# A Strassen-type product of seven blocks for half of the second MLP matrix, with strips and column groups in turn

## The chip, the cores and the metric

One core of a Trainium2 chip runs the whole program. The metric is the device time of one execution in microseconds; lower is better. The kernel before takes 2650.49 us (median of three runs, 2650.14 to 2651.08).

## What is computed

Two transformer-like blocks on 256 tokens of width 2048, in fp32. The change touches only the MLP of the first:

```
ff = square(relu(h @ mlp_w1 + mlp_b1))          # 256 x 2048 by 2048 x 8192
h  = layer_norm(ALPHA * h + ff @ mlp_w2 + mlp_b2)   # 256 x 8192 by 8192 x 2048
```

Ahead of it stand a recurrent and a convolutional mixer; behind it attention, a convolution and a second, gated MLP.

## The kernel before

fp32 accuracy comes from splitting. Every operand a is rounded to `hi` (type fp32r, which TensorE takes in one pass) and `lo` = a - `hi`; a product is `hi*hi + hi*lo + lo*hi`, three passes added up in PSUM. The activations are split once, the weights as they stream through.

**The ring of weights.** A *piece* is 128 x 1024 weights, 512 KB. Four slots (`RING`) hold a raw, a high and a low copy: `w_raw`, `w_hi`, `w_lo`. Piece r (0 to 3) of *quad* q goes through slot r: SyncE loads it (`quad`, L284) once `lo` of the piece before in that slot is done; ScalarE rounds it (`split`, L889 in the rows) once it has landed and TensorE has left the slot (`pe_piece`); VectorE subtracts (`lo`, L1373); TensorE waits for both (`piece_ready`) and counts `pe_piece` up at the end. Every engine takes its work strictly in the order written out by hand in its block.

**The MLP** takes quads 74 to 137, in eight rounds i of 8 quads (`mlp`, on TensorE L652, with functions of the same name on ScalarE and VectorE). A round makes 1024 hidden features and multiplies them with 1024 rows of the second matrix, W2:

- two *strips* of 512 features, 8 pieces each (`strip`): weights are stationary, 512 columns (the tokens' `hi` and `lo`) pass for `w_hi` (L395) and 256 for `w_lo` (L406). Strip k=0 is summed in PSUM half GB, k=1 in GA. At its end ScalarE copies the `lo` part (`halves`, L900, into `half`), VectorE adds it, the rest and the bias (L1777, four steps), squares (L1783), ScalarE rounds (`hi_of`, L904, into `ff`) and VectorE subtracts (`lo_of`, L1397);
- four *column blocks* n of W2, 512 columns each (`token_pieces`, L504 to L506): `ff` of 128 features by 128 tokens is stationary, 512 columns of a piece pass. A piece is two feature tiles of one n, so 2 tiles x 2 token halves x 3 = 12 passes. Each n has two banks (`W2_BANKS`), 8 feature tiles and four pieces; two n share two quads. At the end VectorE adds the banks to `zt` (`add_tokens`, L1766).

In round 0 TensorE also turns the start values of `zt` between the column pieces (`turn_seed`), which ScalarE keeps (`keep_seed`). After the last round come the statistics of the norm (`strip_stats`), a few passes on zeros (`keep_busy`), the turning of the result, and strip 138.

## Time and profile before

| | us |
|---|---|
| median of 3 runs | 2650.49 |
| profiled execution, first to last instruction | 2647.7 |
| MLP, first strip to last column block (trace) | about 893 to 1597 |
| TensorE busy | 2631.6 |
| VectorE busy | 1745.8 |
| ScalarE busy | 1362.4 |

PE is TensorE's matmul, PEld its weight loads (they overlap matmuls), DVE is VectorE, ACT ScalarE, POOL GpSimd, SP SyncE. The matmul ends are modelled (a pass shown as 0.39 us is followed by the next after less), so the distance between starts is what a pass costs. The same holds for VectorE: the next instruction starts a little before the shown end of the one before, unless it must wait for its result. "Idle before <-X" names what an engine waited for.

### The profile page before, as it was taken

To read this page: it belongs to the slowest core of one execution; us is meant where nothing else is said; L and a number is where in the kernel's file an instruction comes from. 1 tells how busy PE (TensorE), PEld (TensorE's weight loads), DVE (VectorE), ACT (ScalarE), POOL (GpSimd) and SP (SyncE) were. 2 spreads that over 40 slices of the span, in tenths; PEclk is the share of its full clock that TensorE was granted. 3 is DMA by queue.
4 is the path that set the end of the run, shared out by engine and by line. 5 is a ranking of instruction groups with operands and counts; after the bars stand their busy time and mean duration, and the time that the engine had idled before them with its cause. 6 is when DMAs were issued, how large, how long until landed. Compare 5 with 4: busy or idle time off the path is not lost.

```text
span 2647.7 us, 40522 instructions
## 1 busy us (share of the span) xinstructions
PE 2631.6 (99%) x14379; PEld 2279.8 (86%) x14379; DVE 1745.8 (66%) x1863; ACT 1362.4 (51%) x1588; POOL 36.1 (1%) x30
## 2 busy tenths in 40 slices
PE   9999999999999999999999999999999999999999
PEld 8888888888888888888888888878888888888888
DVE  7787877544455655555555568996666666666667
ACT  5767765444444544444444445587554444444444
POOL 0000000000000100000000001000100000000000
PEclk9999999999999999999999999999999999999999
DMA  7555555555656455556555664534555555555554
GB/s 266 181 186 184 191 186 195 197 182 189 201 198 199 160 187 193 176 192 202 192 178 193 198 195 153 177 129 147 171 191 190 188 186 188 190 190 190 190 190 168
DMA packets 133881, 494.01 MB, mean 187 GB/s; under 512 B 14864, under 2 KB 15376, under 8 KB 133776
## 3 DMA queue, kind: packets, MB, share of 16 engines
q1 hardware_dynamic: 133776, 492.62, 56.4%
q8 instruction: 65, 1.06, 0.2%
q14 instruction: 40, 0.33, 0.0%
HBM read 490.46 MB, written 2.10 MB: 186 GB/s over the span
## 4 chain that ended last, share of the span: by engine, by line
PE 92%; DVE 3%; ACT 2%; issue 2%; DMA 0%; DVEq 0%; SPq 0%; ACTq 0%
PE ps_b L395 18%; PE ps_a L395 18%; PE ps_b L406 10%; PE ps_a L406 10%; PE ps_b L504 6%; PE ps_b L506 6%; PE ps_b L505 6%; PE ps_a L505 5%; PE ps_a L504 5%; PE ps_a L506 5%; DVE w_lo L1373 1%; PE ps_b L826 1%; ACT w_hi L889 1%; DVE bconv L1874 1%; DVE gates L1519 1%
## 5 line engine op out<-in xcount | busy, mean ns | idle before, releaser
L1373 DVE TENSOR_TENSOR w_lo<-w_raw,w_hi 128x1024 fp32r<-128x1024 f32 (+1 forms) x908 | 1120.4, 1251 | 726.3 <-ACT w_hi L889 716.9
L889 ACT ACTIVATE w_hi<-w_raw 128x1024 fp32r<-128x1024 f32 (+1 forms) x908 | 966.9, 1075 | 1105.1 <-PE ps_a L506 237.1
L395 PE MATMUL ps_b<-xx,w_hi 128*128 128x512 f32 x1184 | 287.9, 392 | 4.0 <-DVE xx L1690 2.3
L395 PE MATMUL ps_a<-xx,w_hi 128*128 128x512 f32 x1120 | 269.1, 391 | 0.0
L395 PEld LDWEIGHTS ps_b<-xx,w_hi 128*128 128x128 f32 x1184 | 216.9, 188 | 47.7 <-ACT w_hi L889 3.7
L395 PEld LDWEIGHTS ps_a<-xx,w_hi 128*128 128x128 f32 x1120 | 205.8, 188 | 39.8
L395 PE MATMUL ps_a<-x,w_hi 128*128 128x512 f32 x704 | 165.9, 390 | 0.0
L395 PE MATMUL ps_b<-x,w_hi 128*128 128x512 f32 x704 | 165.5, 390 | 0.0
L406 PEld LDWEIGHTS ps_b<-xx,w_lo 128*128 128x128 f32 x1184 | 153.2, 192 | 5.8
L406 PE MATMUL ps_b<-xx,w_lo 128*128 128x256 f32 x1184 | 156.0, 284 | 0.0
L395 PEld LDWEIGHTS ps_b<-x,w_hi 128*128 128x128 f32 x704 | 130.8, 188 | 26.2
L395 PEld LDWEIGHTS ps_a<-x,w_hi 128*128 128x128 f32 x704 | 130.6, 188 | 26.1
L406 PEld LDWEIGHTS ps_a<-xx,w_lo 128*128 128x128 f32 x1120 | 142.3, 191 | 4.4
L406 PE MATMUL ps_a<-xx,w_lo 128*128 128x256 f32 x1120 | 144.4, 283 | 0.0
L504 PE MATMUL ps_b<-w_hi,xx 128*128 128x512 f32 (+1 forms) x320 | 122.6, 383 | 0.0
L506 PE MATMUL ps_b<-w_hi,xx 128*128 128x512 f32 (+1 forms) x320 | 121.3, 379 | 0.0
L505 PE MATMUL ps_b<-w_lo,xx 128*128 128x512 f32 (+1 forms) x320 | 121.3, 379 | 0.0
L504 PE MATMUL ps_b<-w_hi,ff 128*128 128x512 f32 x256 | 99.9, 390 | 0.0
L506 PE MATMUL ps_b<-w_hi,ff 128*128 128x512 f32 x256 | 99.6, 389 | 0.0
L505 PE MATMUL ps_b<-w_lo,ff 128*128 128x512 f32 x256 | 99.6, 389 | 0.0
L504 PE MATMUL ps_a<-w_hi,ff 128*128 128x512 f32 x256 | 99.6, 389 | 0.0
L505 PE MATMUL ps_a<-w_lo,ff 128*128 128x512 f32 x256 | 99.6, 389 | 0.0
(305 smaller groups left out, 3933.5 us busy)
## 6 DMA issues: line engine op xcount, KB each, us to landing
w_raw<-w_dram SPq DMA_DIRECT2D x836, 512.0 KB, 3.4
w_raw<-w_dram SPq DMA_DIRECT2D x72, 640.0 KB, 3.9
zz<-x_dram SPq DMA_DIRECT2D x8, 256.0 KB, 4.6
x_res<-x_dram SPq DMA_DIRECT2D x4, 512.0 KB, 6.0
out_dram<-res SPq DMA_DIRECT2D x3, 512.0 KB, 2.8
out_dram<-res SPq DMA_DIRECT2D x4, 128.0 KB, 2.1
const<-const_dram SPq DMA_DIRECT2D x1, 449.0 KB, 4.5
prm<-prm_dram SPq DMA_DIRECT2D x1, 308.0 KB, 5.4
```

What stands on the lines that cost most here:

```text
L395: last = nc.tensor.matmul(group[:, j, :], w_hi[:, r, o * P:o * P + P], moving(src, at + k), start=begins and k == 0, stop=not begins and k ...
L406: last = nc.tensor.matmul(group[:, j, 0:S], w_lo[:, r, o * P:o * P + P], moving(src, at + k)[:, 0:S], start=begins and k == 0, stop=not be ...
L504: nc.tensor.matmul(dst, x_hi, hi, start=k == 0 and not begun, stop=False)
L505: nc.tensor.matmul(dst, x_hi, lo, start=False, stop=False)
L506: last = nc.tensor.matmul(dst, x_lo, hi, start=False, stop=k == kt - 1)
L826: nc.tensor.matmul(banks[:, j // 2, (j % 2) * S:(j % 2) * S + S], w_hi[:, r, cols], mix_tile(k)[:, half_at:half_at + S], start=False, stop ...
L889: act.activation(w_hi[:, r, 0:width], w_raw[:, r, 0:width], ACT.Copy).then_inc(hi_done, 1)
L1373: dve.tensor_tensor(w_lo[:, r, 0:width], w_raw[:, r, 0:width], w_hi[:, r, 0:width].bitcast(F32), ALU.subtract).then_inc(lo_even if r % 2 = ...
L1519: own.done(dve.tensor_tensor_scan(gates[:, hd, way, 0, order], aa[:, way, hd, order], tt[:, way, hd, order], 0.0, ALU.mult, ALU.add))
L1874: ins = dve.scalar_tensor_tensor(y, x, column("cv_w", n), y, ALU.mult, ALU.add)
```

## The change

In rounds i = 1 to 6, and for the second pair of column blocks of round 0, the feature tiles 2 to 5 of the 8 are no longer multiplied block by block. Two feature tiles x two token halves on the left, two feature tiles x two column blocks (two whole pieces) on the right make a 2 x 2 by 2 x 2 block product, done with seven block products instead of eight (`seven_products`, called twice in each `grouped`: g=0 for tiles 2, 3 in slots 2 and 3 of the first quad, g=1 for tiles 4, 5 in slots 0 and 1 of the second). Each block product is three passes of 512 columns. Tiles 0, 1, 6, 7 go as before, before and after. Four results (m1, m5, m6, m7) are summed in GB, and per group added to `q_acc`; m2, m3, m4 go straight into the banks of the plain products in GA. `combined` puts `q_acc` into `zt` once for each pair, at the end.

The sums of blocks that this needs:

- of weights, on VectorE (`mixed_pieces`): a sum of 512 written over the first half of the odd raw piece, a difference of 512 and a difference of 1024, to `t_raw`; then ScalarE rounds 1536 elements (`t_high`) and VectorE subtracts (`t_low`), twice a group;
- of `ff`, four of 256 elements once a round (`next_inputs_of`), rounded and subtracted (`s_hi`, `s_lo`).

The order changes too. A pair of column blocks (a *group*: the 8 pieces of two quads) and a strip alternate, strips are always in GB (but for strip 76), and the strips are made one half round ahead. A strip waits until `q_acc` has taken the group's results out of GB (`q_kept`); a group's seven products wait until the strip's sums are out. The loads come in another order (`by_groups`), with the same bytes. VectorE's order in a group is that of `strip_end` and `group_end`. Round 7 has plain products from its own `ff_last`. GpSimd clears `q_acc` once.

```diff
+        t1_made, t_made, t_hi, t_lo, t_used = (sem(n) for n in ("t1_made", "t_made", "t_hi", "t_lo", "t_used"))
+        s_made, s_hi, s_lo = sem("s_made"), sem("s_hi"), sem("s_lo")
+        q_zero, q_out, q_kept = sem("q_zero"), sem("q_out"), sem("q_kept")
...
+        def product_operands(g, wh, wl, r0, buf):
+
+            r1, k = 2 * (r0 // 2) + 1, 2 * g + 2
+
+            def tile(k, t):
+                return ff[:, k, t * P:t * P + P], ff[:, k, S + t * P:S + t * P + P]
+
+            def summed(n):
+                return s_hi_of[:, n, g * P:g * P + P], s_lo_of[:, n, g * P:g * P + P]
+
+            def piece(r, h):
+                return wh[:, r, 512 * h:512 * h + 512], wl[:, r, 512 * h:512 * h + 512]
+
+            def mixed_piece(n):
+                return thi[:, buf, 512 * n:512 * n + 512], tlo[:, buf, 512 * n:512 * n + 512]
+
+            return dict(m1=(GB[:, 0, :], tile(k, 0), piece(r0, 0)),
+                        m2=(GA[:, 0, :], tile(k + 1, 0), piece(r0, 1)),
+                        m3=(GA[:, 2, :], summed(3), piece(r1, 1)),
+                        m4=(GA[:, 1, :], tile(k + 1, 1), mixed_piece(2)),
+                        m5=(GB[:, 1, :], summed(0), piece(r1, 0)),
+                        m6=(GB[:, 2, :], summed(1), mixed_piece(0)),
+                        m7=(GB[:, 3, :], summed(2), mixed_piece(1)))
 
...
+
+            strip_quads(74, 224)
+            strip_quads(76, 232)
+            strip_quads(78, 256)
+            strip_quads(80, 240)
+            strip_quads(82, 264)
+            by_groups(84, 248)
+            strip_quads(86, 288)
+            with sp.Fori(0, 5) as i:
+                q, at = 8 * i + 88, 32 * i + 256
+                by_groups(q, at + 16)
+                strip_quads(q + 2, at + 40)
+                by_groups(q + 4, at + 24)
+                strip_quads(q + 6, at + 64)
+            by_groups(128, 432)
+            strip_quads(130, 456)
+            by_groups(132, 440)
+            with sp.Fori(0, 8) as i:
+                quad(i + 134, w8, 4 * i + 464, N8)
...
+            def up_strip(q, e, free):
+                strip(q, e, GB, xx, KT, nothing, free=free, by_pairs=True)
+
+            def product(operands, begins, ends):
+
+                bank, (a_hi, a_lo), (b_hi, b_lo) = operands
+                nc.tensor.matmul(bank, a_hi, b_hi, start=begins, stop=False)
+                nc.tensor.matmul(bank, a_hi, b_lo, start=False, stop=False)
+                return nc.tensor.matmul(bank, a_lo, b_hi, start=False, stop=ends)
+
+            def seven_products(i, g, done, q, r0):
+
+                m = product_operands(g, w_hi, w_lo, r0, g)
+                piece_ready(q, r0)
+                product(m["m1"], g == 0, g == 1)
+                product(m["m2"], False, False).then_inc(pe_piece, 1)
+                piece_ready(q, r0 + 1)
+                product(m["m5"], g == 0, g == 1)
+                product(m["m3"], False, False).then_inc(pe_piece, 1)
+                pe.wait_ge(t_hi, done + g + 1)
+                pe.wait_ge(t_lo, done + g + 1)
+                product(m["m6"], g == 0, g == 1)
+                last = product(m["m7"], g == 0, g == 1)
+                if g == 1:
+                    last.then_inc(q_out, 1)
+                product(m["m4"], False, False).then_inc(t_used, 1)
+
+            def grouped(i, pair, q):
+
+                n = 2 * i + pair
+                need = need_ff(2 * i)
+                for nn in range(2):
+                    pe.wait_ge(acc_out, 2 * n - 1 + nn)
+                    token_pieces([(q, nn, two_tiles(0))], sums_of(nn), ff, 8, need)
+                pe.wait_ge(strip_out, outs(E_MLP + 2 * i + 3 + pair))
+                pe.wait_ge(s_hi, i + 1)
+                pe.wait_ge(s_lo, i + 1)
+                seven_products(i, 0, 2 * n - 2, q, 2)
+                need(4)
+                seven_products(i, 1, 2 * n - 2, q + 1, 0)
+                for nn in range(2):
+                    token_pieces([(q + 1, 2 + nn, two_tiles(6))], sums_of(nn), ff, 8, nothing)
...
+            def mlp(i):
+
+                q, e = 8 * i + 80, E_MLP + 2 * i + 3
+                grouped(i, 0, q)
+                up_strip(q + 2, e, lambda: pe.wait_ge(q_kept, 4 * i))
+                grouped(i, 1, q + 4)
...
+            strip(74, E_MLP, GB, xx, KT, need_normed(0), free=lambda: pe.wait_ge(z_kept, 3), turns=False)
+            strip(76, E_MLP + 1, GA, xx, KT, nothing)
+            up_strip(78, E_MLP + 2, lambda: pe.wait_ge(strip_out, outs(E_MLP + 1)))
+            pe.wait_ge(strip_out, outs(E_MLP + 2))
+            in_order(80, sums_of, ff, need_ff(0), beside=seeds_beside)
+            up_strip(82, E_MLP + 3, lambda: pe.wait_ge(seed_kept, 4))
+            grouped(0, 1, 84)
+            up_strip(86, E_MLP + 4, lambda: pe.wait_ge(q_kept, 2))
+            with pe.Fori(0, 5) as i:
                 mlp(i + 1)
-
...
+            mlp(6)
+            pe.wait_ge(q_kept, 26)
+            in_order(134, lambda nn: W2_BANKS[nn], ff_last, need_ff(14))
+            in_order(136, sums_of, ff_last, nothing, begin=lambda nn: pe.wait_ge(acc_out, 27 + nn), apart=z_half)
+
+            pe.wait_ge(acc_out, 30)
...
+            def split_group(n, q, r0):
+
+                split(q, r0)
+                act.wait_ge(t1_made, n + 1)
+                split(q, r0 + 1)
+
+            def t_high(n, buf):
+                hi_of(thi[:, buf, :], t_raw[:, buf, :], t_made, n + 1, t_hi)
+
+            def ff_high(dst, i, k):
+                hi_of(dst[:, 4 * k:4 * k + 4, 0:S], hid[:, k, :, :], ff_made, 2 * i + k + 1, ff_hi)
+
+            def strip_end(q, e, k, sums, n):
+
+                splits(q + 2, N8, (0, 1))
+                split_group(n, q + 2, 2)
+                if sums is not None:
+                    act.wait_ge(s_lo, sums + 1)
+                halves(e, 4 * q + 8, GB)
+                t_high(n, 0)
+
+            def group_end(q, n):
+
+                split_group(n + 1, q + 1, 0)
+                t_high(n + 1, 1)
+                splits(q + 1, N8, (2, 3))
+                splits(q + 2)
+
+            def next_inputs_of(i):
+
                 for k in range(2):
...
+                act.wait_ge(s_made, i + 1)
+                act.activation(s_hi_of, half[:, :, :], ACT.Copy).then_inc(s_hi, 1)
+
+            def mlp(i):
+
+                q, n = 8 * i + 80, 4 * i - 2
+                group_end(q, n)
+                splits(q + 3)
+                strip_end(q + 2, E_MLP + 2 * i + 3, 1, None, n + 2)
+                group_end(q + 4, n + 2)
+
...
+            def mixed_pieces(n, q, r0, buf):
+
+                even, odd = w_raw[:, r0, 0:N8], w_raw[:, r0 + 1, 0:N8]
+                made = t_raw[:, buf, :]
+                dve.wait_ge(raw_in[r0], 16 * q + 16)
+                dve.wait_ge(raw_in[r0 + 1], 16 * q + 16)
+                dve.tensor_tensor(odd[:, 0:512], even[:, 0:512], odd[:, 0:512], ALU.add).then_inc(t1_made, 1)
+                if not (isinstance(n, int) and n < 2):
+                    dve.wait_ge(t_used, n - 1)
+                dve.wait_ge(t1_made, n + 1)
+                own.done(dve.tensor_tensor(made[:, 0:512], odd[:, 0:512], odd[:, 512:N8], ALU.subtract))
+                own.need()
+                dve.tensor_tensor(made[:, 512:1536].rearrange("p (h c) -> p h c", h=2),
+                                  even.rearrange("p (h c) -> p h c", h=2),
+                                  made[:, 0:512].unsqueeze(1).to_broadcast([P, 2, 512]), ALU.subtract).then_inc(t_made, 1)
+
+            def t_low(n, buf):
+                lo_of(tlo[:, buf, :], t_raw[:, buf, :], thi[:, buf, :], n + 1, t_hi, t_lo)
...
+            def strip_end(q, i, k, n):
+
+                e = E_MLP + 2 * i + k
+                los(q + 2, N8, (0, 1))
+                mixed_pieces(n, q + 2, 2, 0)
+                lo(q + 2, 2)
+                activated(e, i, k, GB)
+                lo(q + 2, 3)
+                squared(e + 1, k)
+                t_low(n, 0)
+
+            def group_end(q, pair, n, done):
+
+                mixed_pieces(n + 1, q + 1, 0, 1)
+                los(q + 1, N8, (0, 1))
+                t_low(n + 1, 1)
+                los(q + 1, N8, (2, 3))
+                los(q + 2, N8, (0, 1))
+                dve.wait_ge(q_out, done + 1)
+                for h in range(2):
+                    dve.tensor_tensor(q_acc[:, pair, 2 * h:2 * h + 2, :], GB[:, 2 * h:2 * h + 2, :],
+                                      q_acc[:, pair, 2 * h:2 * h + 2, :], ALU.add).then_inc(q_kept, 1)
+                lo(q + 2, 2)
+                add_sums(pair, 0, 4 * q + 7)
+                lo(q + 2, 3)
+                add_sums(pair, 1, 4 * q + 8)
+
+            def next_inputs_of(i, q):
+
+                dve.wait_ge(ff_made, 2 * i + 2)
+                h = pairs[:, 1:3, :, :, :]
+                one, two, three_, four = (s_sum[:, n, :, :] for n in range(4))
+                own.done(dve.tensor_tensor(one, h[:, :, 0, 1, :], h[:, :, 1, 1, :], ALU.add))
+                own.need()
+                own.done(dve.tensor_tensor(two, one, h[:, :, 0, 0, :], ALU.subtract))
+                own.need()
+                own.done(dve.tensor_tensor(three_, h[:, :, 0, 1, :], h[:, :, 0, 0, :], ALU.subtract))
+                dve.tensor_tensor(four, h[:, :, 1, 0, :], two, ALU.subtract).then_inc(s_made, 1)
+                ff_low(ff, i, 0)
+                lo(q + 1, 0)
+                ff_low(ff, i, 1)
+                lo(q + 1, 1)
+                lo_of(s_lo_of, half[:, :, :], s_hi_of, i + 1, s_hi, s_lo)
+                los(q + 1, N8, (2, 3))
...
+            def combined(pair):
+
+                q = q_acc[:, pair, :, :]
+                dve.wait_ge(q_kept, 24 + 2 * pair)
+                dve.wait_ge(acc_out, 26 + 2 * pair)
+                own.done(dve.tensor_tensor(q[:, 2, :], q[:, 0, :], q[:, 2, :], ALU.add))
+                own.need()
+                own.done(dve.tensor_tensor(q[:, 3, :], q[:, 2, :], q[:, 3, :], ALU.add))
+                own.need()
+                own.done(dve.tensor_tensor(zt[:, :, 2 * pair, :], zt[:, :, 2 * pair, :], q[:, 0:4:3, :], ALU.add))
+                own.need()
+                own.done(dve.tensor_tensor(q[:, 2:4, :], q[:, 1:2, :].to_broadcast([P, 2, 512]), q[:, 2:4, :], ALU.subtract))
+                own.need()
+                own.done(dve.tensor_tensor(zt[:, :, 2 * pair + 1, :], zt[:, :, 2 * pair + 1, :], q[:, 2:4, :], ALU.add))
...
+            def mlp(i, between=None):
+
+                q, n = 8 * i + 80, 4 * i - 2
+                group_end(q, 0, n, 2 * i - 1)
+                if between is not None:
+                    between()
+                los(q + 3)
+                strip_end(q + 2, i + 1, 1, n + 2)
+                group_end(q + 4, 1, n + 2, 2 * i)
...
+            lo(82, 0)
+            dve.wait_ge(seed_kept, 1)
+            add_sums(0, 0, 4 * 81 + 2)
+            los(82, N8, (1, 2))
+            dve.wait_ge(seed_kept, 2)
+            add_sums(0, 1, 4 * 82)
+            lo(82, 3)
+            los(83)
+            dve.wait_ge(seed_kept, 4)
+            strip_end(82, 1, 1, 0)
+            dve.wait_ge(q_zero, 1)
+            group_end(84, 1, 0, 0)
+            next_inputs_of(1, 86)
+            strip_end(86, 2, 0, 2)
+            with dve.Fori(0, 5) as i:
+                own.enter(i, 7)
                 mlp(i + 1)
-            mlp(7, last=True)
+                next_inputs_of(i + 2, 8 * i + 94)
+                strip_end(8 * i + 94, i + 3, 0, 4 * i + 6)
+                own.leave(5)
+            ff_low(ff_last, 7, 0)
+
+            def first_pair():
+                combined(0)
+
+            mlp(6, first_pair)
+            ff_low(ff_last, 7, 1)
...
+            lo(136, 0)
+            add_last(0, None, 4 * 135 + 2)
+            los(136, N8, (1, 2))
...
                 last.then_inc(res_seed, 1)
+            pool.wait_ge(seed_kept, 4)
+            pool.memset(q_acc[:, :, :, :], 0.0).then_inc(q_zero, 1)
```

## Rows read from the trace of the kernel before

**Rows 1.** The page: busy time of each engine, share of the span, instructions

```profile
PE 2631.6 (99%) x14379; PEld 2279.8 (86%) x14379; DVE 1745.8 (66%) x1863; ACT 1362.4 (51%) x1588; POOL 36.1 (1%) x30
```

**Rows 2.** Stretches: length, busy time (instructions) by engine, granted clock, DMA share, GB/s

```profile
core 0: us, PE busy (x) PEld busy (x) DVE busy (x) ACT busy (x) POOL busy (x), PEclk, DMA share, GB/s
...
1152.00:1240.00 88.00, 88.00 (x450) 75.44 (x449) 50.78 (x49) 37.05 (x36) 0.00 (x0) 1.00 0.58 190
```

**Rows 3.** Waits from 896 to 1600: who for whom, total, times, longest

```profile
DVE w_lo L1373 <- ACT w_hi L889: 233.1, 132, 3.4
ACT w_hi L889 <- PE ps_a L506: 102.7, 62, 3.0
```

**Rows 4.** Timeline of PE, 1240 to 1285: start, length, line, operation, count

```profile
1239.64 0.39 PE L506 MATMUL ps_a<-w_hi,ff 128*128 128x512 f32 x1
...
1245.08 0.39 PE L506 MATMUL ps_a<-w_hi,ff 128*128 128x512 f32 x1
1245.30 3.79 PE L395 MATMUL ps_b<-xx,w_hi 128*128 128x512 f32 x16
...
1267.53 3.79 PE L395 MATMUL ps_a<-xx,w_hi 128*128 128x512 f32 x16
```

**Rows 5.** Timeline of DVE at the end of that strip; in brackets idle before

```profile
1269.90 1.66 DVE L1777 SCALAR_TENSOR_TENSOR hid<-ps_b,prm,half 128x256 f32<-128x256 f32 x4 [1.58 <-ACT half L900]
1271.48 1.22 DVE L1373 TENSOR_TENSOR w_lo<-w_raw,w_hi 128x1024 fp32r<-128x1024 f32 x1
1272.61 1.22 DVE L1783 SCALAR_TENSOR_TENSOR hid<-hid 128x1024 f32<-128x1024 f32 x1
...
1298.33 3.49 DVE L1373 TENSOR_TENSOR w_lo<-w_raw,w_hi 128x1024 fp32r<-128x1024 f32 x3
```

**Rows 6.** Timeline of DVE, 1592 to 1599: steps that need the one before

```profile
1592.03 1.23 DVE L1766 TENSOR_TENSOR zt<-ps_a,zt 128x1024 f32<-128x1024 f32 x1 [0.41 <-PE ps_a L506]
1593.29 1.29 DVE L1663 BATCH_NORM_STATS2 stats<-zt 128x6 f32<-128x512 f32 x2
...
1597.46 0.69 DVE L1766 TENSOR_TENSOR zt<-ps_a,zt 128x512 f32<-128x512 f32 x1 [0.28 <-PE ps_a L506]
1598.19 0.69 DVE L1663 BATCH_NORM_STATS2 stats<-zt 128x6 f32<-128x512 f32 x1
```

**Rows 7.** Groups by shape, whole span: count, busy us, mean ns, idle before

```profile
L1373 DVE TENSOR_TENSOR w_lo<-w_raw,w_hi 128x1024 fp32r<-128x1024 f32 x836 | 1014.4, 1231 | 659.1 <-ACT w_hi L889 651.6 <-DVE hid L1385 3.4 <-DVE padded L1385 1.9
L1373 DVE TENSOR_TENSOR w_lo<-w_raw,w_hi 128x1280 fp32r<-128x1280 f32 x72 | 106.1, 1490 | 67.2 <-ACT w_hi L889 65.3 <-issue 1.7
...
L1397 DVE TENSOR_TENSOR xx<-zz,xx 128x512 fp32r<-128x512 f32 x8 | 5.5, 686 | 2.6 <-ACT xx L908 2.6
...
L1397 DVE TENSOR_TENSOR mixc<-ps_a,mixc 128x256 fp32r<-128x256 f32 x8 | 3.4, 419 | 0.0
...
L889 ACT ACTIVATE w_hi<-w_raw 128x1280 fp32r<-128x1280 f32 x72 | 91.7, 1274 | 98.2 <-PE ps_a L506 52.9 <-PE ps_a L448 11.1 <-PE ps_b L448 9.3
```

**Rows 8.** Timeline of ACT at the end of the same strip

```profile
1267.79 1.06 ACT L889 ACTIVATE w_hi<-w_raw 128x1024 fp32r<-128x1024 f32 x1 [0.81 <-PE ps_b L395]
1268.75 1.01 ACT L900 ACTIVATE half<-ps_b 128x1024 f32<-128x1024 f32 x1
```

**Rows 9.** Timeline, 1608 to 1612: TensorE stands and starts again

```profile
1609.87 1.67 DVE L1690 SCALAR_TENSOR_TENSOR xx<-res,prm,xx 128x256 fp32r<-128x256 f32 x4
...
1611.69 0.70 PE L395 MATMUL ps_b<-xx,w_hi 128*128 128x512 f32 x2 [2.31 <-DVE xx L1690]
```

**Rows 10.** DMA issues by tile: count, KB each, median us to landing

```profile
w_raw<-w_dram SPq DMA_DIRECT2D x836, 512.0 KB, 3.4
```

**Rows 11.** Stretches around that start, columns as in rows 2

```profile
1612.00:1614.00 2.00, 2.00 (x8) 1.60 (x7) 2.00 (x2) 2.00 (x5) 0.00 (x0) 0.77 0.00 0
1614.00:1616.00 2.00, 2.00 (x11) 1.99 (x10) 1.85 (x5) 0.99 (x2) 0.00 (x0) 0.50 0.77 268
1616.00:1618.00 2.00, 2.00 (x13) 1.82 (x12) 0.82 (x2) 1.06 (x1) 0.00 (x0) 0.87 0.74 231
```

More of the change, by code:

```diff
@@ new lines, in in_order @@
+            def in_order(q, banks, src, need, begin=None, beside=None, apart=None):
+                for c in range(2):
+                    for nn in range(2):
+                        if c == 0 and begin is not None:
+                            begin(nn)
+                        pieces = [(q + c, 2 * nn + h, two_tiles(4 * c + 2 * h)) for h in range(2)]
+                        if apart is not None and (c, nn) == (1, 1):
+                            token_pieces(pieces, banks(nn), src, 8, need, apart)
+                            continue
+                        for _, r, runs in pieces:
+                            if beside is not None:
+                                beside(c, r)
+                            token_pieces([(q + c, r, runs)], banks(nn), src, 8, need)
@@ new lines, in mlp @@
+            def mlp(i):
[4 more added lines that the diff above has]
+                group_end(q + 4, n + 2)
+            splits(76)
+            halves(E_MLP, 4 * 74 + 8, GB)
+            splits(77)
+            splits(78)
+            halves(E_MLP + 1, 4 * 76 + 8, GA)
+            next_inputs_of(0)
+            splits(79)
+            splits(80)
+            act.wait_ge(s_lo, 1)
@@ new lines, in _ @@
+            halves(E_MLP + 2, 4 * 78 + 8, GB)
+            splits(81, N8, (0, 1))
+            keep_seed(0)
+            split(81, 2)
+            keep_seed(1)
+            split(81, 3)
+            split(82, 0)
+            keep_seed(2)
+            split(82, 1)
+            keep_seed(3)
+            splits(82, N8, (2, 3))
+            splits(83)
+            strip_end(82, E_MLP + 3, 1, None, 0)
+            group_end(84, 0)
+            next_inputs_of(1)
+            splits(87)
+            strip_end(86, E_MLP + 4, 0, 1, 2)
@@ new lines, in t_low, with activated @@
+            def t_low(n, buf):
+                lo_of(tlo[:, buf, :], t_raw[:, buf, :], thi[:, buf, :], n + 1, t_hi, t_lo)
+            def activated(e, i, k, group):
+                dve.wait_ge(half_out, e + 1)
+                for j in range(SN):
+                    ins = dve.scalar_tensor_tensor(hid[:, k, j, :], group[:, j, 0:S],
+                                                   column("b1", 4 * k + j + 8 * i), half[:, j, :], ALU.add, ALU.add)
+                ins.then_inc(strip_out, 1)
```

235 lines of the change are left out of this document (105 added, 130 removed).

## The prediction

> **What bounds the kernel now.** I read the busy table first: TensorE is busy for 99% of the span [rows 1], so every pass taken away is worth its length if nothing takes its place. The stretch table then shows a steady stretch of the MLP, 88 us, one round of two strips and four W2 column blocks: TensorE is busy throughout at granted clock 1.00, VectorE for 50.78 us (58%), ScalarE for 37.05 us [rows 2]. The waits between 896 and 1600 us hold no row of TensorE; what waits is VectorE for `w_hi` (233.1 us in all), and ScalarE for TensorE to give a slot back [rows 3]. So VectorE has spare time on average. Whether it has some at the place where the change needs it is the question, and the timelines answer that.
>
> The clock of the sum: from the start at 1239.64 to that at 1245.08 lie 24 passes of 512 columns [rows 4], so one pass is 5.44 / 24 = 0.2267 us. A strip goes from 1245.30 to 1267.53, 22.23 us [rows 4]. A pair of column blocks (8 pieces of 12 passes, quads q and q+1) is 96 x 0.2267 = 21.76 us. Strip and pair together are 43.99 us, and two of these are 88.0 us, the round.
>
> **What goes away.** `seven_products` has 7 x 3 passes for two pieces instead of 24, and each `grouped` call has two of it: 6 passes less, 90 instead of 96, 1.36 us. `grouped` runs 13 times (`grouped(0, 1)`, and twice each for i = 1 to 6); i = 7 and the first pair of i = 0 keep eight products. TensorE's work shrinks by 78 x 0.2267 = 17.7 us. The order of strips and groups, the loads (same bytes, other order), `w_hi` and `w_lo` stay otherwise.
>
> **What VectorE gets.** Prices are distances from start to start: a 1024-element difference costs 1.135 us in a run (3.50 us for three, the last counted with its 1.23 in full) [rows 5]. A step that needs the result before it starts after the whole duration: a 512-element one 0.73 us later (1597.46 to 1598.19), a 1024-element one 1.26 us [rows 6]. For 1536 elements there is no row. The nearest are 128x1024 with 1.231 and 128x1280 with 1.490 us [rows 7]; from 512 to 1024 the slope gives 1.231 + 0.545 = 1.78, from 1024 to 1280 1.75. Bounds: 1.490 below (a bit more than 1280 elements), 2 x 1.231 above; I take 1.77, that is 1.675 to the next start. One such step stands in the chain below, 13 times in all: the lower end would make the time 3.6 us shorter, the upper 9.0 us longer, and the range holds both. `mixed_pieces` is 0.73 + 0.73 + 1.14 = 2.60 us, and a pair has two; `t_low` 1.675, two; `q_acc` two PSUM additions of 1.14 us; `next_inputs_of` four sums of 256 elements, 0.42 us long each [rows 7], and one `s_lo`. A strip with its group comes to 16 x 1.135 (the `lo`), 1.58 + 1.14 (bias, square), 5.20, 3.35, 2.27, 2.27 (adding into `zt`) and half of 5.0 (`next_inputs_of`, once in two): 37.5 us of 42.6, or 88%. On average that fits. ScalarE gets two `t_high` and half an `s_hi`, about 3.4 us in 42.6; it has room.
>
> **Where it doesn't fit.** Let T be TensorE's first pass after a strip (1267.53 in the trace). VectorE can't take the strip's sums before ScalarE has `half`: split at 1267.79, `half` at 1268.75, VectorE's first bias step at 1269.90 [rows 5, 8], T + 2.37. That won't move, since in `strip_end` the split of the last slot stands before `halves` as before. From there, in the order of `strip_end` and `group_end`: four bias steps 1.58, `lo(q+2, 3)` 1.13, square 1.14, `t_low` 1.675, `mixed_pieces` of the second block set 2.60, then `lo` of that set's first piece, 1.23 to its end. That is T + 2.37 + 9.36 = 11.73, and TensorE starts again some 0.15 us after VectorE's end (1609.87 + 1.67 = 11.54 against 11.69 [rows 9]): T + 11.88. TensorE wants this piece after two plain pieces and seven products, 24 + 21 = 45 passes: T + 10.20. It stands still for 1.68 us, and behind that `piece_ready` all of its later work is queued.
>
> The other waits of the group: the first `t_low` ends at T + 7.99, wanted at 36 passes = T + 8.16: just in time, and if it slips, that only eats into the 1.68. The second goes at 12.78 (ScalarE's `t_high` before it, from 10.7 to about 12.2, by 1.27 us for 1280 elements [rows 7]) and ends at 14.54, wanted at 11.88 + 12 passes = 14.60; with 0.15 to resume this is a stall of 0.09. `lo` of slots 2 and 3 end at 15.7 and 16.8, wanted at 16.7 and 19.4: nothing. `q_acc` follows two more `lo` and ends near T + 21.35, and the next strip waits for it; TensorE gets there at 11.88 + 0.09 + 45 x 0.2267 = T + 22.17. Nothing, but only 0.8 us of room. In the strip (22.23 us) VectorE has 8 `lo`, the `zt` sums and perhaps `next_inputs_of`; it is through `mixed_pieces` and `lo` of slot 2 by about T + 1.0, before the T + 2.37 at which the chain starts anew. So nothing piles up. Of the four raw blocks loaded in that time the last is issued at about 14 to 15 us into the strip and lands 3.4 us later [rows 10], ahead of its sums at 19.4.
>
> **The sum.** Group before 21.76, after 22.17: +0.41 us. So 13 x 0.41 = +5.3 us: a saving of 17.7 and stalls of 23.0. Once, `combined(1)` (two dependent steps of 0.73, three of 1.26, 5.2 us) stands before quad 135: at the start of quad 134 VectorE still owes 2 `lo`, two sums and an `ff_low`, so the first `lo` of 135 ends 11.3 us in, wanted after 48 passes = 10.9: +0.55. `combined(0)` and the first `next_inputs_of` stand beside strips with 4 us and more to spare: nothing, and were that cover gone, 5 us and 1 us once. Pool's memset stands beside a strip of which VectorE needs `q_acc` only afterwards: nothing, at most its own few us once. Sum +5.9 us on the profiled span of 2647.7; the median of the runs is 2650.49, 2.8 above it, and I carry that over: 2656.4.
>
> A rule against the row: the Trainium skill, VectorE: DVE Perf Modes, Terms, says that a VectorE instruction can't issue until the pipeline of the one before is empty. By it the four bias steps and three big ones of the chain would each be 0.09 us longer, some 0.6 us a group, 8 us in all, and the time 2664. The trace doesn't agree: three steps of 1.23 us take 3.50, not 3.69 [rows 5].
>
> **Rivals.** *A stall that costs the clock (slower).* The trace has one idle stretch of 2.31 us before 1611.69, and right behind it the granted clock is 0.77 and then 0.50, the lower of the levels 1.2 and 2.4 GHz, where it was 1.00 before; it is back at 1.00 by 1618 [rows 9, 11]. The clock was short by 2 x (0.23 + 0.50 + 0.13), 1.7 us. If my 1.68 us stalls do that in half of the groups, 6.5 x 1.7 = 11 us more: 2667; in each, 2678. Against it: the stall is shorter and dense passes stand on both sides. The Trainium skill, TensorE: Matmul & The Clock Gate, HAM oscillation, has the same rule, that an idle gap inside a loop throttles again each round; the trace agrees for its one gap. The same event at the end of the MLP may also come or stay away, 1.7 us.
> *The strip waits for `q_acc` (slower).* SyncE issues the first piece of the next strip only after that late `lo`; if blocks land over 4.5 us after issue instead of the 3.4 of the median, `lo` of slots 0 and 1 and with them `q_acc` slip past T + 22.1. At 5 us it is 0.5 us a group: 2663.
> *The saving is kept (faster).* If VectorE reached the second set's `lo` 1.5 us earlier (steps on SBUF alone cheaper than I price them, by half), nothing would stall but the 21.4 us of `q_acc`, 0.4 us better than before a group: 2646; with that gone too, 2633. Against it: rows on SBUF and on PSUM cost the same 1.22 to 1.23 us, and all of the chain's first half is in the trace. In between lies a part: each step 0.05 us cheaper, 2650.
>
> **How the numbers follow.** About 0.2% (5.3 us, so 2645.2 to 2655.8) is what a measurement of this kernel can tell from no change. My chain as it stands, 2653 to 2660: 0.60, of which 0.25 within 0.2%. Clock: 0.10. `q_acc`: 0.10. Saving kept: 0.10 faster. The part in between: 0.10, same. So faster 0.10, same 0.35, slower 0.55. Range 2648 to 2668: it leaves out the kept saving and the worst of the clock.
>
> **What would show it.** TensorE's waits should name VectorE's `w_lo` 13 times, 1.4 to 1.9 us each, at the first pass of the second block set, and `tlo` with 0.2 us or less. Groups should be 22.2 us from strip end to strip start, with VectorE without a gap from T + 2.4 to T + 21. If groups are near 20.4 us, my chain is wrong; if waits on `q_acc` or DMA lead, the second rival is right; if passes of 0.43 us stand behind the stalls, the first.

## The result

The changed kernel takes 2663.95 us (median of 4, 2661.97 to 2665.61), the kernel before beside it 2650.31 us (2649.03 to 2651.08): ratio 1.0051, 95% interval 1.0037 to 1.0066, so 13.6 us slower. The direction was forecast and the time lies in the range (2648 to 2668). The size was not: +5.9 us were forecast, and the 2653 to 2660 that the prediction gave to its main line, the chain on VectorE, was missed too.

The page of the changed kernel, busy times (columns as in [rows 1]) and then two stretches of the steady part (columns as in [rows 2]):

```profile
span 2663.8 us, 40298 instructions
...
PE 2625.3 (99%) x14301; PEld 2262.6 (85%) x14301; DVE 1903.8 (71%) x2031; ACT 1403.6 (53%) x1621; POOL 39.8 (1%) x31
```

```profile
1152.00:1240.00 88.00, 86.00 (x434) 72.44 (x435) 72.02 (x73) 42.80 (x41) 0.00 (x0) 1.00 0.58 191
1240.00:1328.00 88.00, 85.22 (x431) 71.44 (x430) 72.09 (x72) 42.21 (x40) 0.00 (x0) 1.00 0.59 191
```

TensorE has 14301 passes instead of 14379, the 78 that were to go, and now has holes: 85 to 86 us busy of 88, where [rows 2] has 88. VectorE went from 50.78 to 72 us of 88. The granted clock is 1.00 as before.

Waits of TensorE in the MLP (896 to 1625), where [rows 3] has none:

```profile
PE ps_b L730 <- DVE w_lo L1552: 19.0, 13, 2.6
PEld ps_b L730 <- DVE w_lo L1552: 17.8, 10, 1.8
...
PE ps_b L464 <- DVE q_acc L2001: 1.4, 3, 0.9
```

L730 is the first pass of a block product, L1552 `lo`. There are 13 waits, one for each group, as forecast. One of them in the timeline of TensorE, T = 1230.14 (first pass after the strip; L573 to L575 plain passes, L730 to L732 block products, L464 the next strip):

```profile
1230.14 0.39 PE L573 MATMUL ps_a<-w_hi,ff 128*128 128x512 f32 x1
...
1240.23 0.40 PE L732 MATMUL ps_a<-thi,ff 128*128 128x512 f32 x1
1242.01 0.50 PE L730 MATMUL ps_b<-w_hi,ff 128*128 128x512 f32 x1 [1.38 <-DVE w_lo L1552]
1242.35 0.39 PE L731 MATMUL ps_b<-w_lo,ff 128*128 128x512 f32 x1
...
1247.07 0.39 PE L573 MATMUL ps_a<-w_hi,ff 128*128 128x512 f32 x1
...
1252.28 0.39 PE L575 MATMUL ps_a<-w_hi,ff 128*128 128x512 f32 x1
1252.75 3.93 PE L464 MATMUL ps_b<-xx,w_hi 128*128 128x512 f32 x16
```

TensorE starts again at T + 11.87; the prediction had T + 11.88. VectorE in the same group:

```profile
1232.57 1.66 DVE L1968 SCALAR_TENSOR_TENSOR hid<-ps_b,prm,half 128x256 f32<-128x256 f32 x4 [1.50 <-ACT half L1028]
1234.14 1.22 DVE L1552 TENSOR_TENSOR w_lo<-w_raw,w_hi 128x1024 fp32r<-128x1024 f32 x1
1235.28 1.22 DVE L1974 SCALAR_TENSOR_TENSOR hid<-hid 128x1024 f32<-128x1024 f32 x1
1236.41 1.75 DVE L1576 TENSOR_TENSOR tlo<-t_raw,thi 128x1536 fp32r<-128x1536 f32 x1
1238.08 0.69 DVE L1951 TENSOR_TENSOR w_raw<-w_raw 128x512 f32<-128x512 f32 x1
1238.87 0.69 DVE L1955 TENSOR_TENSOR t_raw<-w_raw 128x512 f32<-128x512 f32 x1
1239.60 1.22 DVE L1957 TENSOR_TENSOR t_raw<-w_raw,t_raw 128x1024 f32<-128x1024 f32 x1
1240.74 2.35 DVE L1552 TENSOR_TENSOR w_lo<-w_raw,w_hi 128x1024 fp32r<-128x1024 f32 x2
1243.01 1.75 DVE L1576 TENSOR_TENSOR tlo<-t_raw,thi 128x1536 fp32r<-128x1536 f32 x1
1244.68 3.49 DVE L1552 TENSOR_TENSOR w_lo<-w_raw,w_hi 128x1024 fp32r<-128x1024 f32 x3
1249.11 1.22 DVE L1552 TENSOR_TENSOR w_lo<-w_raw,w_hi 128x1024 fp32r<-128x1024 f32 x1 [0.94 <-ACT w_hi L1017]
1250.25 2.35 DVE L2001 TENSOR_TENSOR q_acc<-ps_b,q_acc 128x1024 f32<-128x1024 f32 x2
```

Read it from the top: the four bias steps, the last plain `lo`, the square, `t_low`, the three sums of weights, and only then the `lo` for which TensorE stands. One step hands over to the next with no idle time until 1248.17. The price taken for 1536 elements (1.77) measured 1.75.

**Where the 13 us are.** From the end of strip 76 (934.26 before, 935.73 after) to where TensorE takes up strip 138 again (1611.69 [rows 9], 1626.26 after) it is 677.43 us before and 690.53 after: 13.1 us more. (The two profiled executions are 16.1 us apart. Of the other 3.0 us, 1.5 lie in the first 200 us and 1.5 behind this stage, where the changed kernel's trace has a stretch at low clock that the other trace has not; the last section comes back to it. The change touches neither part, and the medians are 13.6 us apart.) Starts of passes cut each period into four stretches: 24 plain passes, the block stretch (42 passes, 9.52 us at 0.2267), 24 plain passes, the strip (22.23 us [rows 4]). The table sums over all groups what each kind of stretch lasts beyond this length, its own length below:

| | us, all groups | forecast |
|---|---|---|
| 78 passes gone | -17.7 | -17.7 |
| block stretches (11.27 to 11.49, one 12.61) | +25.6 | +23.0 |
| last plain stretches (up to 6.53 instead of 5.44) | +3.0 | 0 |
| strips (22.32 to 22.37 in 8 of 12) | +1.0 | 0 |
| quad 134 (12.07 instead of 10.88) | +1.2 | +0.55 |
| sum | +13.1 | +5.9 |

The stretch of 12.61 stands behind this (VectorE's timeline, then TensorE's):

```profile
1504.81 1.75 DVE L1576 TENSOR_TENSOR tlo<-t_raw,thi 128x1536 fp32r<-128x1536 f32 x1
1506.48 1.22 DVE L1576 TENSOR_TENSOR ff_last<-hid,ff_last 128x1024 fp32r<-128x1024 f32 x1
1507.62 0.69 DVE L1951 TENSOR_TENSOR w_raw<-w_raw 128x512 f32<-128x512 f32 x1
```

```profile
1511.64 0.47 PE L730 MATMUL ps_b<-w_hi,ff 128*128 128x512 f32 x1 [2.60 <-DVE w_lo L1552]
```

`ff_low(ff_last, 7, 0)` stands between the last `strip_end` and `group_end`, inside the chain. The prediction overlooked it. It costs its own 1.14 us once. The pause is 2.60 us here, and the granted clock stays at 1.00 behind it.

### The profile page after: what moved, and what is told of

It is laid out like the page before. It is cut to its first block, busy times and chain, and to the rows that moved or that the text cites. A ratio compares the mean times of both kernels' runs of the same rounds, so it can differ in the third digit from the quotient of the medians.

```text
span 2663.8 us, 40298 instructions
## 1 busy us (share of the span) xinstructions
PE 2625.3 (99%) x14301; PEld 2262.6 (85%) x14301; DVE 1903.8 (71%) x2031; ACT 1403.6 (53%) x1621; POOL 39.8 (1%) x31
## 4 chain that ended last, share of the span: by engine, by line
PE 85%; DVE 7%; ACT 3%; issue 3%; DMA 1%; DVEq 0%; SPq 0%; ACTq 0%
PE ps_b L464 22%; PE ps_a L464 14%; PE ps_b L475 11%; PE ps_a L475 7%; PE ps_a L574 4%; PE ps_a L575 4%; PE ps_a L573 4%; PE ps_b L573 4%; PE ps_b L575 4%; PE ps_b L574 4%; DVE w_lo L1552 2%; ACT w_hi L1017 1%; DMA w_raw<-w_dram 1%; DVE tlo L1576 1%; PE ps_b L954 1%
## 5 line engine op out<-in xcount | busy, mean ns | idle before, releaser
L1552 DVE TENSOR_TENSOR w_lo<-w_raw,w_hi 128x1024 fp32r<-128x1024 f32 (+1 forms) x908 | 1117.9, 1250 | 606.8 <-ACT w_hi L1017 597.8
L464 PE MATMUL ps_b<-xx,w_hi 128*128 128x512 f32 x1632 | 395.2, 393 | 5.7 <-DVE xx L1869 2.3
L464 PEld LDWEIGHTS ps_b<-xx,w_hi 128*128 128x128 f32 x1632 | 300.1, 189 | 68.7 <-issue 5.8
L475 PE MATMUL ps_b<-xx,w_lo 128*128 128x256 f32 x1632 | 211.4, 283 | 0.0
L464 PE MATMUL ps_a<-x,w_hi 128*128 128x512 f32 x704 | 165.9, 390 | 0.0
L464 PE MATMUL ps_b<-x,w_hi 128*128 128x512 f32 x704 | 165.5, 390 | 0.0
L464 PE MATMUL ps_a<-xx,w_hi 128*128 128x512 f32 x672 | 163.7, 392 | 0.0
L464 PEld LDWEIGHTS ps_b<-x,w_hi 128*128 128x128 f32 x704 | 130.8, 188 | 26.2
L464 PEld LDWEIGHTS ps_a<-x,w_hi 128*128 128x128 f32 x704 | 130.7, 188 | 26.1
L464 PEld LDWEIGHTS ps_a<-xx,w_hi 128*128 128x128 f32 x672 | 122.7, 189 | 23.1
L573 PE MATMUL ps_b<-w_hi,xx 128*128 128x512 f32 (+1 forms) x320 | 123.3, 385 | 0.0
L575 PE MATMUL ps_b<-w_hi,xx 128*128 128x512 f32 (+1 forms) x320 | 121.9, 381 | 0.0
L573 PE MATMUL ps_a<-w_hi,ff 128*128 128x512 f32 x240 | 93.8, 391 | 0.0
L575 PE MATMUL ps_a<-w_hi,ff 128*128 128x512 f32 x240 | 93.5, 389 | 0.0
L475 PEld LDWEIGHTS ps_a<-xx,w_lo 128*128 128x128 f32 x672 | 86.7, 191 | 4.4 <-DVE w_lo L1552 1.0
L475 PEld LDWEIGHTS ps_a<-x,w_lo 128*128 128x128 f32 x704 | 87.8, 192 | 1.9
L475 PE MATMUL ps_a<-xx,w_lo 128*128 128x256 f32 x672 | 89.0, 283 | 0.3 <-DVE w_lo L1552 0.3
L475 PEld LDWEIGHTS ps_b<-x,w_lo 128*128 128x128 f32 x704 | 87.4, 192 | 1.7
```

The costliest lines, as they stand in the source:

```text
L464: last = nc.tensor.matmul(group[:, j, :], w_hi[:, r, o * P:o * P + P], moving(src, at + k), start=begins and k == 0, stop=not begins and k ...
L475: last = nc.tensor.matmul(group[:, j, 0:S], w_lo[:, r, o * P:o * P + P], moving(src, at + k)[:, 0:S], start=begins and k == 0, stop=not be ...
L573: nc.tensor.matmul(dst, x_hi, hi, start=k == 0 and not begun, stop=False)
L575: last = nc.tensor.matmul(dst, x_lo, hi, start=False, stop=k == kt - 1)
L1552: dve.tensor_tensor(w_lo[:, r, 0:width], w_raw[:, r, 0:width], w_hi[:, r, 0:width].bitcast(F32), ALU.subtract).then_inc(lo_even if r % 2 = ...
```

## Experiments

Two questions: is it the place of VectorE's work that costs (the chain), its amount, or the new order; and what makes up the part that was not forecast? The figures under "stretches" are means over ten periods from about 1050 us on, from starts of passes, in the order plain, block, plain, strip; the sum is one strip with its group (43.99 before the change). The thirteenth group and the plain quads behind it are not in these means, and e5 has no block products.

| kernel | stretches, us | sum | median, us | before beside it | ratio, 95% interval |
|---|---|---|---|---|---|
| changed | 5.44, 11.41, 5.68, 22.33 | 44.86 | 2663.95 | 2650.31 | 1.0051 (1.0037 to 1.0066) |
| e1_square_later | 5.44, 10.31, 5.77, 22.36 | 43.88 | 2649.88 | 2649.85 | 1.0000 (0.9990 to 1.0010) |
| e2_sums_ahead | 6.28, 9.66, 5.44, 22.23 | 43.61 | 2646.29 | 2649.85 | 0.9987 (0.9978 to 0.9997) |
| e4_small_sums | 5.44, 9.62, 5.44, 22.28 | 42.78 | 2634.28 | 2649.85 | 0.9940 (0.9924 to 0.9957) |
| e5_order_alone | | | 2649.98 | 2649.85 | 1.0001 (0.9991 to 1.0011) |
| e7_extra_in_chain | 5.44, 13.58, 5.54, 22.26 | 46.82 | 2687.66 | 2649.82 | 1.0141 (1.0126 to 1.0157) |
| e8_extra_in_strip | 5.44, 11.41, 5.57, 22.33 | 44.75 | 2663.84 | 2649.82 | 1.0050 (1.0034 to 1.0065) |
| e3_q_early | 5.44, 11.42, 5.44, 22.23 | 44.53 | 2660.64 | 2649.82 | 1.0040 (1.0027 to 1.0054) |
| e6_sums_split | 5.44, 9.60, 5.67, 22.36 | 43.06 | 2642.29 | 2649.82 | 0.9971 (0.9960 to 0.9982) |
| e9_all | 5.45, 9.62, 5.54, 22.22 | 42.84 | 2636.26 | 2650.40 | 0.9948 (0.9934 to 0.9962) |

### e5_order_alone: the order without the products

```diff
             def seven_products(i, g, done, q, r0):
+                for nn in range(2):
+                    token_pieces([(q, r0 + nn, two_tiles(2 * g + 2))], sums_of(nn), ff, 8, nothing)
-                m = product_operands(g, w_hi, w_lo, r0, g)
...
```

On VectorE and ScalarE `mixed_pieces`, `t_high`, `t_low`, the sums of `ff`, `q_acc` and `combined` are gone.

> The new order alone: strips and groups in turn, all strips but one in GB, loads by groups, with eight plain products everywhere and none of the sums of weights, sums of ff or q_acc. Theories 'chain' and 'total': the order is free, 2650 us. Rival 'order': most of the 13 us, 2658 to 2664, with TensorE waiting at the starts of strips or for w_hi.

Measured 2649.98 us, ratio 1.0001 (0.9991 to 1.0011). The new order of strips, groups and loads costs nothing that can be measured. So the theory that the order costs the time falls.

### e4_small_sums: without the sums of weights

```diff
-dve.tensor_tensor(odd[:, 0:512], even[:, 0:512], odd[:, 0:512], ALU.add)
+dve.tensor_tensor(odd[:, 0:2], even[:, 0:2], odd[:, 0:2], ALU.add)
...
-hi_of(thi[:, buf, :], t_raw[:, buf, :], t_made, n + 1, t_hi)
+hi_of(thi[:, buf, :].rearrange("p (a c) -> p a c", c=P), ones[:, :].unsqueeze(1).to_broadcast([P, 12, P]),
+                      t_made, n + 1, t_hi)
```

> The three weight sums of mixed_pieces cut to two columns, and t_high and t_low take a constant of the same length instead: the sums of weights are left out of what is computed; passes, loads, t_high, t_low, q_acc and every wait stay. It takes 2 x 2.1 us of VectorE's work out of each group, 2.1 of them before the first w_lo of the second set. Theory 'chain': no stall there (9.6 us against 10.2), q_acc near 20.4 us, so the saved passes come through: 2636 us. Rival 'total': 2636 too. Rival 'order': at most the 0.2% of noise, 2660 or more.

Measured 2634.28 us. With the sums of weights left out, and every pass and wait in place, the seven products bring 15.6 us. The block stretch is 9.62 us, and one short wait of TensorE for `lo` is left in the whole stage:

```profile
PE ps_b L730 <- DVE w_lo L1553: 0.5, 1, 0.5
```

### e7_extra_in_chain and e8_extra_in_strip: one more step at two places

```diff
+                dve.tensor_tensor(padded[:, :, 0:S], xx[:, 0:4, 0:S].bitcast(F32), xx[:, 4:8, 0:S].bitcast(F32), ALU.add)
                 mixed_pieces(n + 1, q + 1, 0, 1)
```

```diff
                 add_sums(pair, 1, 4 * q + 8)
+                dve.tensor_tensor(padded[:, :, 0:S], xx[:, 0:4, 0:S].bitcast(F32), xx[:, 4:8, 0:S].bitcast(F32), ALU.add)
```

> The changed kernel with one more VectorE addition of 1024 elements (1.14 us, its result unused) in each of the 13 groups, ahead of mixed_pieces of the second block set, inside the chain. Theory 'chain': 13 x 1.14 = 14.8 us more, 2679, the stall at the second set grows from 1.6 to 2.7 us. Rival 'total': 14.8 too. A theory in which TensorE has room there: 2664.

> The same addition, 13 times, but right behind the two zt sums, early in the strip (or in quad 134 for the last one). Theory 'chain': VectorE has room there and is on time at the strip's end: 2664, at most 1 us more for the last of the 13. Rival 'total': 2679, as e7_extra_in_chain.

The same step, 13 times: 2663.84 us in the strip, no change; 2687.66 us in the chain, 23.7 us more. So the place decides, not the amount. (The thirteenth step of e8 does not stand beside a strip but in quad 134, where VectorE is late already; there TensorE's pause grows from 0.90 to 2.00 us. The twelve beside strips cost nothing.) But 23.7 is more than the 14.8 of the step. Of the twelve block stretches from 1057 us on, three are 12.51 to 12.53 us, which is close to 11.41 + 1.14; eight are 13.94 to 14.10 and one, that with `ff_last`, is 15.01. All thirteen together are 27.8 us longer than in the changed kernel, 14.8 by the step and some 13 by what follows; about 3 us come back, because TensorE waits less behind them. A stretch of 13.94 in the timeline of TensorE, then stretches of 2 us from 1063 on and, for comparison, through one of 12.53 (columns as in [rows 2]):

```profile
1065.13 0.50 PE L730 MATMUL ps_b<-w_hi,ff 128*128 128x512 f32 x1 [2.50 <-DVE w_lo L1552]
...
1066.68 0.63 PE L730 MATMUL ps_b<-w_hi 128*128 128x512 f32 x1
1067.96 0.63 PE L730 MATMUL ps_a<-w_hi 128*128 128x512 f32 x1
1069.24 0.63 PE L730 MATMUL ps_b<-thi,w_hi 128*128 128x512 f32 x1
```

```profile
1063.00:1065.00 2.00, 0.00 (x0) 0.00 (x0) 2.00 (x3) 1.08 (x2) 0.00 (x0) 1.00 0.00 0
1065.00:1067.00 2.00, 1.87 (x7) 1.55 (x8) 2.00 (x3) 2.00 (x3) 0.00 (x0) 0.88 0.39 125
1067.00:1069.00 2.00, 2.00 (x6) 1.52 (x6) 2.00 (x3) 0.95 (x2) 0.00 (x0) 0.50 0.88 250
1069.00:1071.00 2.00, 2.00 (x9) 1.60 (x8) 2.00 (x3) 0.46 (x1) 0.00 (x0) 0.76 0.69 248
...
1112.00:1114.00 2.00, 1.75 (x8) 1.44 (x9) 2.00 (x3) 2.00 (x3) 0.00 (x0) 1.00 0.30 82
1114.00:1116.00 2.00, 2.00 (x10) 1.48 (x9) 2.00 (x2) 0.55 (x2) 0.00 (x0) 1.00 0.75 250
```

Behind the pause of 2.50 us the granted clock falls to 0.50, 1.2 of 2.4 GHz, for some 3 us, and a product's three passes take 1.28 us (1066.68 to 1067.96) instead of 0.68. That is the first rival of the prediction, shown with a longer pause than the change makes: it comes in nine of the thirteen groups, at 1.5 us each. The Trainium skill, TensorE: Matmul & The Clock Gate, HAM oscillation, says that an idle gap inside a loop throttles the engine again each round; this trace agrees for nine of the thirteen pauses and not for the other four, of 2.44 to 2.50 us. In the changed kernel, with twelve pauses of 1.3 to 1.5 us and the one of 2.60, the clock stays at 1.00 through these groups.

### e1_square_later and e2_sums_ahead: the same work at other places

```diff
             def strip_end(q, i, k, n):
...
                 lo(q + 2, 2)
+                mixed_pieces(n + 1, q + 3, 0, 1)
                 activated(e, i, k, GB)
                 lo(q + 2, 3)
-                squared(e + 1, k)
                 t_low(n, 0)
             def group_end(q, pair, n, done, ik):
-                mixed_pieces(n + 1, q + 1, 0, 1)
                 los(q + 1, N8, (0, 1))
                 t_low(n + 1, 1)
+                squared(E_MLP + 2 * ik[0] + ik[1] + 1, ik[1])
```

e1 moves only the square (and `ff_low(ff_last, 7, 0)`), e2 `mixed_pieces` too.

> The changed kernel with the square of the strip's result moved behind the second t_low of the group (and ff_low of ff_last, 1.14 us once in the same chain, moved behind the last first group); same work, same passes. Theory 'chain' (TensorE stands because VectorE's steps between the end of a strip and the first w_lo of the second block set last 11.7 us where 10.2 are there): 1.14 us leave the chain, the stall falls from about 1.6 to 0.4 us; but VectorE is busy without a gap until q_acc, which ends no earlier than 21.4 us after the strip's end, so a group is 21.5 instead of 22.5 us: 2650 us, as before the change. Rival 'total' (VectorE has too much work in all, its place doesn't matter): no change, 2664. Rival 'order' (the new order of strips, groups and loads costs it): no change, 2664.

> As e1_square_later, and mixed_pieces of the second block set (2.60 us) stands before the bias steps, where VectorE waits 1.3 to 1.5 us for ScalarE's half. Same work, same passes. Theory 'chain': from the strip's end 2.6 of 9.4 us more leave the chain, w_lo of the second set is there at about 9 us, wanted at 10.2: no stall; q_acc ends at about 20 us, wanted at 20.4. Groups of 20.4 to 20.8 us: 2637 us. If the second set's raw blocks land late (4.8 us after issue, as some did), the bias steps move back by 1 us and the last plain w_lo with them: 2643. Rivals 'total' and 'order': 2664.

e1: 2649.88 us, as forecast. The block stretch falls by 1.10 us, by what left the chain. 14.1 us are gained by moving one step of 1.14 us in each group and one of 1.14 us once (14 x 1.14 = 16.0).

e2: 2646.29 us, forecast 2637 or 2643. The block stretch is at its own length, but the plain stretch ahead of it is 6.28 instead of 5.44. TensorE's and VectorE's waits there:

```profile
DVE w_raw L1952 <- DMA w_raw<-w_dram: 10.0, 14, 0.9
PE ps_b L730 <- DVE hid L1969: 9.6, 13, 2.0
```

Now the block products wait for the bias steps (L1969), which stand behind sums that wait for their raw blocks. One stall has become another, 0.8 us instead of 1.9. Late blocks were named as a danger, too small. In the last group, which is not in the means, the pause is 1.99 us, and the granted clock falls to 0.50 behind it.

### e3_q_early: the wait at the start of strips

```diff
                 los(q + 1, N8, (2, 3))
-                los(q + 2, N8, (0, 1))
                 dve.wait_ge(q_out, done + 1)
...
+                los(q + 2, N8, (0, 1))
```

> The changed kernel with the additions into q_acc ahead of w_lo of slots 0 and 1 of the next strip, so that they don't wait for late raw blocks. Theory: the waits for q_acc at the starts of strips (2.9 us in all) and the slower strips behind them (about 1 us) go: 2660 us; the stall at the second block set stays. Rival (the next strip then waits for w_hi or w_lo of its first pieces instead): 2664.

Measured 2660.64 us, as forecast: the last plain stretch is 5.44 and the strip 22.23 in the mean, the block stretch is the same 11.42. In the group with `ff_last` TensorE's pause is 2.60 us as in the changed kernel, but here the granted clock fell behind it, and that block stretch took 14.13 us instead of 12.61. TensorE's timeline of e3, then a stretch of 2 us behind the pause (columns as in [rows 2]):

```profile
1508.89 0.72 PE L730 MATMUL ps_b<-w_hi,ff 128*128 128x512 f32 x1 [2.60 <-DVE w_lo L1552]
```

```profile
1510.00:1512.00 2.00, 2.00 (x7) 1.52 (x6) 2.00 (x2) 1.02 (x3) 0.00 (x0) 0.50 0.92 289
```

So the additions into `q_acc` were late because the `lo` in front of them waited. ScalarE's timeline in the changed kernel shows for what (the splits of slots 0, 1 and 2 of the next strip):

```profile
1245.44 1.06 ACT L1017 ACTIVATE w_hi<-w_raw 128x1024 fp32r<-128x1024 f32 x1 [1.20 <-DMA w_raw<-w_dram]
1247.93 1.06 ACT L1017 ACTIVATE w_hi<-w_raw 128x1024 fp32r<-128x1024 f32 x1 [1.43 <-DMA w_raw<-w_dram]
1250.91 1.06 ACT L1017 ACTIVATE w_hi<-w_raw 128x1024 fp32r<-128x1024 f32 x1 [1.92 <-DMA w_raw<-w_dram]
```

Slot 0's `lo` ended at 1241.97 and its next block was there 3.5 us later; slot 1's ended at 1243.09 and its block was there at 1247.9, 4.8 us later. That is the prediction's second rival, at 0.24 us in this group, up to 1.09 us in others, and nothing in the last plain stretch of 6 of 12.

### e6_sums_split and e9_all: towards a version that keeps the saving

```diff
             def strip_end(q, i, k, n):
...
                 lo(q + 2, 2)
+                mixed_pieces(n + 1, q + 3, 0, 1)
                 activated(e, i, k, GB)
...
             def group_end(q, pair, n, done, ik):
-                mixed_pieces(n + 1, q + 1, 0, 1)
+                mixed_rest(0, 1)
```

In these two `mixed_pieces` holds the two sums of 512 elements only, and `mixed_rest` the one of 1024. e9 has e3's order too, and the five steps of `combined` one by one between the `lo` of quads 131 and 135.

> As e2_sums_ahead, but only the two sums of 512 elements (1.46 us) stand ahead of the bias steps, where VectorE has 1.3 to 1.5 us idle, the one of 1024 behind the first t_low. In e2 TensorE waited about 0.8 us a group for the bias steps. Theory 'chain': the bias steps are on time (wanted 5.44 us after the strip's end), w_lo of the second set ends at 9.2 to 9.9 us, wanted at 10.2, the second t_low at 12.0 to 12.7, wanted at 12.9, q_acc at 20.0: groups of 20.5 us, 2635 us. If raw blocks land so late that the bias steps still wait: 2640 to 2644. Rival (something else holds the groups at 21.3 us, as in e2): 2646.

> e6_sums_split and e3_q_early together, and the steps of combined spread between the w_lo of quads 131 and 135 instead of in one piece ahead of them (in e6 the last group still stood 1.5 us for the bias steps and 0.7 us in its block stretch, and quad 134 and 135 about 1 us). Same work, same passes. Theory 'chain': every stretch at its own length, 5.44 + 9.52 + 5.44 us for a group and 22.23 for a strip, so all of the 17.7 us of saved passes comes through: 2633 us. If a rest of 0.3 us a group stays somewhere: 2637. Rival (q_acc early pushes the next strip's first w_lo too late): 2640 to 2644 as e6.

e6: 2642.29 us, 7 us above the forecast. It lies in the 2640 to 2644 that were given for bias steps that still wait for late blocks, but that is not what happened: the stretch ahead of the block products is at its own 5.44. The block stretch is 9.60, so the chain is gone. What is long again is the last plain stretch and the strip (5.67 and 22.36), where the late additions into `q_acc` stand; that they are the reason was not tried on this version by itself. With them early, in e9, the strips are at 22.22 and the last plain stretch is 5.54. e9: 2636.26 us, ratio 0.9948 (0.9934 to 0.9962), the fastest version that computes everything, 14.1 us under the kernel before and 27.7 under the changed one. It does the same work, with the same 78 passes less; 2633 was forecast, or 2637 with a small rest in each group. Its stretch is full again:

```profile
1240.00:1328.00 88.00, 88.00 (x449) 74.99 (x448) 75.58 (x76) 44.34 (x42) 0.00 (x0) 1.00 0.60 197
```

3.6 of the 17.7 us are still out. Starts of passes in its trace show where 3 of them are: the block stretches of the 13 groups are 1.8 us above their own length, 0.7 of it in the last group, and the last plain stretches 1.2 us, 0.10 us a group.

## Why the prediction was right, and where not

- *TensorE bounds, 78 passes go, 17.7 us.* Right: 14301 instead of 14379 passes, and e4 brings 15.6 us.
- *The chain on VectorE.* Right, in its place and to 0.15 us: TensorE resumes at T + 11.73 to 11.87 in the twelve groups without `ff_last` (forecast 11.88), 13 waits on `w_lo`. e1 and e7 move it by the length of the step that is taken out or put in, e8 shows that the same step beside a strip is free, e5 that the order is.
- *Average load is no bound.* Right: VectorE at 72 us of 88 in the changed kernel, at 75.58 us in e9, where TensorE has no pause in that stretch. (The terms named for VectorE's load add up to 36.5 us and not to the 37.5 written, 86% and not 88%; nothing else rests on it.)
- *Block stretch +1.77 us.* Too small by 0.12 us a group: after a wait the first passes are spaced 0.34 and 0.23 to 0.24 us instead of 0.2267 (1242.01, 1242.35, 1242.58 in TensorE's timeline of this group). Two more spacings of about 0.31 us stand in most block stretches, where the first and the second `t_low` are only just in time, as the prediction had them. 1.5 us in all. The step "TensorE starts again 0.15 us after VectorE's end" held in three groups; in the other ten it was 0.05 us (here 1241.96 against 1242.01), and the bias steps began at T + 2.43 here where the prediction had T + 2.37. That these two cancel made the 11.87 look more exact than it was. That TensorE then needs a little longer was not priced.
- *`ff_low(ff_last)`.* Missed, 1.1 us: the list of VectorE's steps was made from `strip_end` and `group_end` and not from the written sequence between them.
- *`q_acc`: nothing, 0.8 us of room.* Wrong by 3.0 us, and 1.0 us of slower strips behind the waits. The step of the prediction that failed is the landing time: 3.4 us from the median of the whole run [rows 10], where blocks asked for within 1.1 us of each other took 3.5 and 4.8. The rival that had it was given one chance in ten, as an either-or at 0.5 us in every group; it came in part, 0.2 us a group in the mean.
- *`combined(1)` +0.55.* It was 1.2. The step that failed is the lead of 0.8 us that VectorE was to have at the start of quad 134. TensorE waited for `q_acc` there, which ends at 1566.98, so both start together and the steps count in full, 5.7 + 5.2 + 1.2 = 12.1 us against 10.9 of passes. TensorE's waits first, then VectorE's steps:

```profile
1567.04 0.50 PE L573 MATMUL ps_b<-w_hi,ff_last 128*128 128x512 f32 x1 [0.39 <-DVE q_acc L2001]
1579.11 0.47 PE L573 MATMUL ps_b<-w_hi,ff_last 128*128 128x512 f32 x1 [0.90 <-issue]
```

```profile
1564.63 2.35 DVE L2001 TENSOR_TENSOR q_acc<-ps_b,q_acc 128x1024 f32<-128x1024 f32 x2
1566.90 1.22 DVE L1552 TENSOR_TENSOR w_lo<-w_raw,w_hi 128x1024 fp32r<-128x1024 f32 x1
...
1572.56 0.69 DVE L2031 TENSOR_TENSOR q_acc<-q_acc 128x512 f32<-128x512 f32 x1
...
1577.79 4.63 DVE L1552 TENSOR_TENSOR w_lo<-w_raw,w_hi 128x1024 fp32r<-128x1024 f32 x4
```

- *The clock.* Rightly left out of the sum for the twelve pauses of 1.3 to 1.5 us. e7 shows that one more step of 1.14 us in the chain would have brought it in. That it stayed away behind the one pause of 2.60 us was luck: e3 has the same pause, and it cost 1.5 us there.
- *The number.* The range held because it left room for rivals, not because the sum was right. Of the 7.5 us between 2656.4 and 2663.95 (7.7 beside the 2650.31 measured with it) the terms above have 7.2 in the trace: 1.5 and 1.1 in the block stretches, 3.0 and 1.0 at and behind the waits for `q_acc`, 0.6 for `combined(1)`.
- *The rule that VectorE drains between steps* (the Trainium skill, VectorE: DVE Perf Modes, Terms) would have made 2664, which is near the measured time, by accident: the timeline has `lo` steps of 1.22 us 1.13 to 1.14 us apart (3.49 us for three), so the 7.7 us lie elsewhere, as the table shows.

## What to carry to other kernels

A saving on the engine that bounds is worth what the engine that feeds it can do between two fixed points, not what it can do on average: write down the serial steps from the event that can't move (here the strip's end) to the first result that is wanted, and compare with the passes in between. Where that fails, look for steps in the chain that nobody wants yet, and for idle time just ahead of the fixed point: moving the square and two of the three sums was worth 21.7 us here (e6), and with the additions into `q_acc` early and the steps of `combined` spread out 27.7 us (e9), with no work taken away. Put steps that free a buffer ahead of steps that may wait for a load.
